# Splitting the expert gathers of a PEER layer into score rows and value rows

## The reference

```python
ue = u[eidx]          # (tokens, heads, 16, 1024): score rows of the chosen experts
ve = v[eidx]          # value rows of the same experts
act = gelu(einsum('td,thkd->thk', xi, ue))
out = einsum('thk,thkd->td', g * act, ve)
```

## Time and profile before

| | |
|---|---|
| median of 3 runs | 1931.69 us (1931.65 to 1932.42) |
| span of the profiled execution | 1928.8 us |
| PE / DVE / ACT / POOL busy | 83% / 52% / 34% / 27% of the span |
| DMA, whole span | 610.20 MB, mean 316 GB/s |
| indirect gathers | 512 of 1 MB, 536.90 MB |

### The profile page before, as it was taken

The page is one execution under the profiler, slowest core; times in us unless marked ns, Lnnn a source line. Parts: engine busy times, 40 slices in busy tenths (PEclk is TensorE's granted clock), DMA queues, the critical chain, the costliest instruction groups (busy, mean ns, idle before and its releaser), DMA issues.

```text
span 1928.8 us, 15560 instructions
## 1 busy us (share of the span) xinstructions
PE 1591.4 (83%) x4638; PEld 806.3 (42%) x4638; DVE 1011.3 (52%) x2487; ACT 646.9 (34%) x1897; POOL 514.9 (27%) x516
## 2 busy tenths in 40 slices
PE   7999989767877877787779989997788777877876
PEld 4777778222322222222237666763232222222222
DVE  3432238688544554445441632489874445444454
ACT  1243221423433333333332433123343333333333
POOL 0000001434433433333300000015444343333331
PEclk9999999999999999999989999999999999999999
DMA  8321224999999999999933222359999999999996
GB/s 304 131 88 44 101 108 184 390 416 421 422 421 422 421 422 422 421 421 422 421 154 131 88 104 93 118 221 422 421 421 421 422 421 421 422 421 422 421 421 287
DMA packets 107540, 610.20 MB, mean 316 GB/s; under 512 B 10032, under 2 KB 10176, under 8 KB 41280
## 3 DMA queue, kind: packets, MB, share of 16 engines
q0 software_dynamic: 73728, 536.90, 67.1%
q1 hardware_dynamic: 33728, 72.30, 10.3%
HBM read 608.12 MB, written 1.05 MB: 316 GB/s over the span
## 4 chain that ended last, share of the span: by engine, by line
DMA 45%; PE 38%; DVE 9%; ACT 5%; issue 2%; POOL 0%; SPq 0%; DVEq 0%; PEldq 0%; ACTq 0%
DMA arena<-in_experts,idxT 45%; PE psum L516 37%; DVE arena L1416 5%; ACT cst L882 1%; ACT gains L882 1%; ACT arena L882 1%; ACT gelus L882 1%; ACT L882 1%; DVE red L1385 1%; DVE kv L1377 0%; POOL arena L1710 0%; DMA vecs<-in_vecs 0%; ACT sqb L882 0%; DVE kv L1383 0%; DVE red L1200 0%
## 5 line engine op out<-in xcount | busy, mean ns | idle before, releaser
L516 PE MATMUL psum<-arena,cst 128*128 128x512 f32 (+2 forms) x2112 | 1029.4, 616 | 283.6 <-ACT cst L882 279.1
L1416 DVE CUSTOM_DVE_ANT_0 arena<-arena,xrow 128x1024 f32<-128x1024 f32 x512 | 624.4, 1224 | 537.7 <-DMA arena<-in_experts,idxT 537.0
L1710 POOL DMA_INDIRECT arena<-in_experts,idxT x512 | 514.7, 1005 | 1387.8 <-PE psum L516 790.0
L516 PEld LDWEIGHTS psum<-arena,cst 128*128 128x128 f32 x2112 | 367.1, 191 | 942.5 <-ACT cst L882 645.7
L882 ACT ACTIVATE gelus<-red 128x1 f32<-128x1 f32 x512 | 103.6, 202 | 770.2 <-DVE red L1416 769.9
L516 PE MATMUL psum<-hT,ring 128*128 128x256 f32 x1280 | 293.3, 390 | 6.1 <-DVE hT L1215 6.1
L516 PEld LDWEIGHTS psum<-hT,ring 128*128 128x128 f32 x1280 | 248.9, 196 | 47.5 <-issue 9.8
L882 ACT ACTIVATE cst<-cst,gains 128x128 f32<-128x128 f32 x512 | 206.2, 403 | 23.2 <-PE psum L516 6.7
L882 ACT ACTIVATE gains<-gelus,gateT 128x1 f32<-128x1 f32 x512 | 150.8, 294 | 17.0 <-ACT gelus L882 0.2
L882 ACT ACTIVATE arena<-psum 128x512 f32<-128x512 f32 (+3 forms) x89 | 47.8, 545 | 304.3 <-PE psum L516 304.0
L516 PE MATMUL psum<-mixT,ring 128*128 128x256 f32 x256 | 57.4, 387 | 2.5 <-DVE mixT L1689 2.5
(11 more groups left out here) (161 smaller groups left out, 672.1 us busy)
## 6 DMA issues: line engine op xcount, KB each, us to landing
ring<-in_peer_wq SPq DMA_DIRECT2D x8, 2048.0 KB, 8.1
ring<-in_ev_w_in SPq DMA_DIRECT2D x6, 2048.0 KB, 11.8
ring<-in_od_w_in SPq DMA_DIRECT2D x5, 2048.0 KB, 33.0
ring<-in_xa_wkv SPq DMA_DIRECT2D x4, 2048.0 KB, 7.9
arena<-in_experts,idxT POOLq DMA_INDIRECT x512, 15.3
ring<-in_ev_w_out SPq DMA_DIRECT2D x2, 2048.0 KB, 7.8
ring<-in_xa_wq SPq DMA_DIRECT2D x2, 2048.0 KB, 9.2
ring<-in_xa_wo SPq DMA_DIRECT2D x2, 2048.0 KB, 7.7
```

The costliest lines, as they stand in the source:

```text
L516: return nc.tensor.matmul(out, lhsT, rhs, start=start, stop=stop)
L1416: V.tensor_tensor_reduce(out=ut, in0=ut, in1=xrow[:, u // PAIRS, :], scale=1.0, scalar=0.0, op0=ALU.mult, op1=ALU.add, accum_out=dots[:, k ...
L1710: nc.gpsimd.indirect_dma_start(slot[slot_of(u)], None, d["experts"], bass.IndirectOffsetOnAxis(ap=idxT[:, u:u + 1], axis=0))\
```

## The change

The table is split into `experts_u` and `experts_v`, with rows of 4 KB. The ring of eight 8 KB slots becomes two rings of eight 4 KB slots: one for score rows, one for value rows. POOL issues two gathers for each unit, 128 rows each, and the score rows run two units ahead (`SCORE_LEAD`). A score slot is free when its unit's dot is done, a value slot when its matmuls are done. DVE waits for score rows alone, PE for its diagonal and the value rows.

```diff
+SCORE_LEAD = 2
-        slot = [arena[:, j * 2 * D:(j + 1) * 2 * D] for j in range(SLOTS)]
+        u_slot = [arena[:, j * D:(j + 1) * D] for j in range(SLOTS)]
+        v_slot = [arena[:, (SLOTS + j) * D:(SLOTS + j + 1) * D] for j in range(SLOTS)]
...
-        def slot_of(u):
-            return (u + 1) % SLOTS
+        def u_of(u):
+            return (u + 2) % SLOTS
+        def v_of(u):
+            return u % SLOTS
+        def scored(eng, l, u):
+            eng.wait_ge(dotted, l * UNITS + u + 1)
...
                         pe.wait_ge(weighed, l * UNITS + u + 1)
-                        v = slot[slot_of(u)][:, D:2 * D]
+                        pe.wait_ge(v_landed[v_of(u)], 16 * ((l * UNITS + u) // SLOTS + 1))
+                        v = v_slot[v_of(u)]
...
                 def unit(u):
-                    landed(dve, l, u)
-                    ut = slot[slot_of(u)][:, 0:D]
+                    dve.wait_ge(u_landed[u_of(u)], 16 * ((l * UNITS + u) // SLOTS + 1))
+                    ut = u_slot[u_of(u)]
...
         @block.gpsimd
         def _(pool):
+            def gather(table, dst, u, landed):
+                nc.gpsimd.indirect_dma_start(dst, None, d[table],
+                                             bass.IndirectOffsetOnAxis(ap=idxT[:, u:u + 1], axis=0)).then_inc(landed, 16)
+
+            def scores(l, u):
+                if u < PAIRS and u % 32 == 0:
+                    pool.wait_ge(idx_ready, 8 * l + u // 32 + 1)
+                if u == PAIRS:
+                    pool.wait_ge(idx_ready, 8 * l + 8)
+                if u == SLOTS - 2:
+                    full(pool, f"ps{l}.7")
+                if u >= SLOTS:
+                    scored(pool, l, u - SLOTS)
+                gather("experts_u", u_slot[u_of(u)], u, u_landed[u_of(u)])
+
+            def values(l, u):
+                if u >= SLOTS:
+                    taken(pool, l, u - SLOTS)
+                gather("experts_v", v_slot[v_of(u)], u, v_landed[v_of(u)])
+
             for l in range(LAYERS):
-                for u in range(UNITS):
-                    if u < PAIRS and u % 32 == 0:
-                        pool.wait_ge(idx_ready, 8 * l + u // 32 + 1)
-                    if u == PAIRS:
-                        pool.wait_ge(idx_ready, 8 * l + 8)
-                    if u == SLOTS - 1:
-                        full(pool, f"ps{l}.7")
-                    if u >= SLOTS:
-                        taken(pool, l, u - SLOTS)
-                    nc.gpsimd.indirect_dma_start(slot[slot_of(u)], None, d["experts"],
-                                                 bass.IndirectOffsetOnAxis(ap=idxT[:, u:u + 1], axis=0))\
-                        .then_inc(gathered[slot_of(u)], 16)
+                for u in range(UNITS + SCORE_LEAD):
+                    if u < UNITS:
+                        scores(l, u)
+                    if u >= SCORE_LEAD:
+                        values(l, u - SCORE_LEAD)
```

More of the change, by code:

```diff
@@ L399, in trunk @@
         idx_ready = sem("idx_ready")
-        gathered = [sem(f"gathered{j}") for j in range(SLOTS)]
+        u_landed = [sem(f"u_landed{j}") for j in range(SLOTS)]
+        v_landed = [sem(f"v_landed{j}") for j in range(SLOTS)]
         dotted = sem("dotted")
@@ L445, in trunk @@
         HEAD = {"x0": 0, "m": XA_H, "x1": XA_H + MO_H}
-        def slot_of(u):
-            return (u + 1) % SLOTS
-        def landed(eng, l, u):
-            eng.wait_ge(gathered[slot_of(u)], 16 * (l * UNITS // SLOTS + u // SLOTS + 1))
+        def u_of(u):
[4 more added lines that the diff above has]
+            eng.wait_ge(dotted, l * UNITS + u + 1)
         def taken(eng, l, u):
@@ L1766 @@
         "subkeys": np.ascontiguousarray(sub).reshape(LAYERS, PE_DQ, 16 * PE_KEYS),
-        "experts": np.concatenate([a["peer_u"].reshape(-1, D), a["peer_v"].reshape(-1, D)], 1),
+        "experts_u": np.ascontiguousarray(a["peer_u"].reshape(-1, D)),
+        "experts_v": np.ascontiguousarray(a["peer_v"].reshape(-1, D)),
     }
```

## The result

The changed kernel takes **1997.53 us** (median of 4 runs, 1985.68 to 2014.59) against 1932.06 us of the kernel before beside it (1931.65 to 1933.96): 1.0344 times, 95% interval 1.0287 to 1.0401. The profiled execution took 2004.74 us with a span of 2002.9, which is 74.1 us over the span before. The prediction was 2002 us, 1955 to 2105.

The account below looks back on a forecast made before the run. DMA engines bound the kernel before; after the split, POOL would. Layers of 680 us in place of 637.4 and 653.3 add 70 us to the 1928.8 us span, and with 2.9 us around it give 2002 us, range 1955 to 2105.

Parts of the forecast that it names:

- POOL issues twice: POOL's two gathers a unit: 1.24 us each (0.94 busy, 0.30 issue), 2.48 us a unit against 2.485 of DMA.
- A gather that finds a dot running waits: POOL beside DVE's dot: a gather starting during a dot is held until 1.09 us after the dot's start, then takes 0.94.
- Routing stretch: Gathers beside DVE's routing, up to unit 76's score rows: POOL bounds, 142 gathers at 1.445 us, 205 us a layer.
- the step that scaled the hold with DVE's busy share: Beside the routing: mean hold per gather scaled from 0.25 us by 0.68 / 0.83 to 0.205 us.
- Quiet stretch: Units after the routing: POOL, held by dots, needs 2.60 us a unit; 179 units take 465 us a layer.
- (a): Layer's end: with value rows last, the last unit's matmuls start at the landing, 2.3 us less for each layer.
- (b): Score slots freed by the dot, not the matmuls: nothing in steady state, at most 4.5 us gained in the second layer.
- (c): Layer's start: ten half gathers instead of seven whole ones come first, moving two units, 5.0 us, into each layer's block.
- The sum: A layer: 205 + 465 + 3.7 value gathers + 4.1 landing + 2.0 matmuls = 680 us; +70 for both layers.
- The price of 4 KB rows: DMA engines: 149 ns a mean packet, at most +5.9%; at +3% a unit takes 2.56 to 2.59 us, hidden behind POOL.
- D: Rival for the whole kernel: POOL isn't held or keeps up, only the 4 KB rows cost; 1971 us, 10%.
- C: Rival for the units after the routing: a worse phase of holds, 2.75 to 2.95 us a unit, 2055 to 2127 us; 20%.

Follow-up runs that it names:

- experiment 5: Changed kernel with tables of 2 KB rows, the dot taking the tokens for both inputs and half of each value row used twice: 2165.28 us.
- Experiment 6: Changed kernel limited to seven gathers in flight: 2037.56 us with the real dot, 1975.71 us with a one-input sum; unedited beside them 1996.1 us.
- experiment 4: Kernel before with each layer's last four units gathered apart, score rows one unit ahead: 1929.95 us; also the changed kernel, unedited, again: 2116.28 us.
- chip R: Third chip of the follow-ups: kernel before 1928.52 us, changed kernel unedited 1996.1 us, with one-input sum and at most seven gathers in flight 1975.71 us.

## Why the prediction was right

- **POOL issues twice, 1.24 us each.** Right, and by rows, not bytes: 0.94 + 0.30 with 8, 4 and 2 KB rows.
- **A gather that finds a dot running waits until 1.09 us after its start.** Right in both directions: with the one-input sum a gather takes 0.94 us in the mean, and the held gather of experiment 5 ends within 0.02 of the sum. The Trainium skill ("SBUF — State Buffer", section "Who interferes with whom") names two SBUF inputs as the condition; the trace agrees, since with one input the mean of all gathers falls from 1.03 to 0.94.
- **Routing stretch 205 us.** Measured 206.8 and 201.5. The mean gather there is 1.14 us against the 1.145 used (0.94 + 0.205), so the step that scaled the hold with DVE's busy share held too. The count was off by two: from unit 6's score gather to unit 76's there are 70 + 70 = 140 gathers, not 142, and 140 x 1.445 is 202 us. In the first layer there are 4.5 us more, which the sum doesn't have; its DMA engines were at 390 GB/s with a share of 1.01 in this stretch, against 359 and 0.96 in the second, so the weights that the prediction fitted into idle DMA time are the likely cause; no run tests it.
- **Quiet stretch, 2.60 us a unit.** The number is right (179 units took 465.9 and 463.3 us, 465 predicted), its cause only for a part. Up to about 700 us POOL and its holds set 2.6 to 2.7 us (385 and 398 GB/s). After that the DMA engines do, at 2.56, and the hold only fills what POOL has left. So the number is in part luck: two limits within 2% of each other. The prediction had that price (+3%, 2.56 to 2.59) and called it hidden behind POOL's 2.60; it is the other way about. Experiment 6 prices the hold in this stretch at nothing. The landing is 6.6 us and not 4.1, and the DMA share 1.03 and not under 1.0: the queue isn't empty, and the gather that a dot holds comes three periods behind that dot's own score gather and not two. The estimate of 2.57 us from the Trainium skill ("DMA: Bandwidth & Descriptors", section "iDMA fabric — 4 AXI ports for 8 engines, asymmetric across TPBs") was the better guide: its 408.7 GB/s for 4 KiB rows stand against 409 here, by POOL or by SP.
- **(a) 2.3 us at a layer's end.** Mis-sized: 1.7 and 1.3 us in experiment 4, where the last two units' matmuls stand behind each other. In the sum itself the end of a layer was put at 3.7 + 4.1 + 2.0 = 9.8 us and took 13.4: the landing is 2.5 us longer, and three units' matmuls stand behind each other (5.39 us) where one unit's were counted. (b) and (c) can't be told apart in the profile.
- **The sum.** 680 us a layer; measured 686.1 and 678.2. +70 predicted, +74.1 in the span of the profiled run, +65.5 in the medians. Two small errors, three us too many by the count of gathers and 3.6 too few at the end, cancel in it.
- **The price of 4 KB rows.** The line through two packet times gave 149 ns for a mean packet, and that is what it is (68.5% of 16 x 2002.9 us over 147456). The +5.9% that was read from it as the upper bound isn't the rate's, which fell by 3%, as the busy share rose from 1.01 to 1.03.
- **The rivals.** D's account (only the rows cost, 1971) had its 2.56 us, but POOL set the pace beside the routing as well: without holds it is 1976 on chip R, where it is 1996 with them. C (a worse phase, from 2055) didn't come in the first timings, but experiment 5 shows its mechanism at 2.98 us, with 2 KB rows, and experiment 6 longer holds at up to 2.80. That the same program took 2116 us on another occasion is outside the range and in none of the cases: there the prediction would have been wrong. It took the profile of one occasion to stand for all, and that the first timing fell on a short one is luck.

## What to carry to other kernels

Before a gather is split, divide the path by rows and not by bytes: the issuing engine pays for each 128 rows again, here 1.24 us, and a kernel that was bound by transfers at 2.49 us had just that slack and no more. Once the issuing engine is near the pace, whatever holds it now and then (here a two-input dot on the same memory) becomes part of the period, and through the landing it sets its own phase, which a small edit can make worse (here from 1996 to 2038 us). And a kernel that takes the same time on every occasion can become, by such a change, one that doesn't: time it on more than one.

## What was not expected of the hardware

- 4 KB rows move at 409 GB/s where 8 KB rows move at 422, from POOL's queue alone or from two queues: 2.56 against 2.485 us for 1 MB.
- The hold feeds itself through the landing, and with half the bytes a unit was longer: 2.98 us with 2 KB rows against 2.56 with 4 KB.
- With 4 KB rows the program came to rest in two phases, score gathers held or value gathers held, with the same hold of 0.07 us and the same 409 GB/s.
- One and the same program at 1997.53, 2116.28 and 1996.1 us, each within 1.5% in itself, where the kernel before took 1928.5 to 1932.1 us in the median each time. In the long one ACT waits up to 8.3 us at a time, PE idles, and the granted clock is 0.934 over the span against 0.984.
